# A mixture-of-experts layer on one core: expert rows written plainly to a place of their own, with an eleventh weight buffer

## What is computed

```python
x = x + concat(y_ssd, y_s5) @ w_out                  # x1 below
x = x + _hier_moe(_rmsnorm(x, norm_ffn), ...)        # then a final RMSNorm

def _hier_moe(x, ...):       # coarse top-1 of 4 groups, top-2 of the 8 experts inside it
    ...
    for e in range(32):      # w_gate, w_up: 1024 x 512, w_down: 512 x 1024, each 2 MB
        h = silu(t @ w_gate[e]) * (t @ w_up[e])
        out = out + gates[:, e:e + 1] * (h @ w_down[e])
```

## Time and profile before

| | us |
|---|---|
| runs before, three | 1048.75, 1051.2, 1053.29; median 1051.2 |
| the profiled execution, its own time | 1051.08 |
| its span, first to last instruction | 1049.2 |
| TensorE matmuls busy | 935.7 (89%) |
| VectorE, ACT, POOL busy | 434.6, 329.4, 269.8 |
| data moved by DMA | 276.98 MB, mean 264 GB/s |
| mean granted TensorE clock | 0.983 of full speed |

### The profile page before, as it was taken

One profiled execution on the slowest core, in us unless ns is written; L12 is line 12 of the kernel. 1 busy time (PEld: TensorE's weight loads), 2 busy tenths in 40 slices (PEclk: granted clock), 3 DMA queues, 4 the chain that ended last, 5 costly groups with the idle time before them and its releaser, 6 DMA issues. The chain is left out here.

```text
span 1049.2 us, 17043 instructions
## 1 busy us (share of the span) xinstructions
PE 935.7 (89%) x6336; PEld 668.2 (64%) x6337; DVE 434.6 (41%) x759; ACT 329.4 (31%) x670; POOL 269.8 (26%) x511
## 2 busy tenths in 40 slices
PE   6999999999999999999899999998778777887880
PEld 5889778877786789998765555554344343444440
DVE  6999977344557879763531111110110101110112
ACT  3025323453324785223212322222212112122125
POOL 1000788888521010000022222222112121122112
PEclk9999999999999999999999999999999999999995
DMA  7586073121099748375699999999999999999984
GB/s 271 122 141 99 24 121 89 41 63 42 31 178 221 233 141 320 90 259 201 245 354 366 376 394 392 374 402 392 385 405 408 388 406 410 412 413 415 425 346 164
DMA packets 86815, 276.98 MB, mean 264 GB/s; under 512 B 37272, under 2 KB 55576, under 8 KB 69872
## 3 DMA queue, kind: packets, MB, share of 16 engines
q1 hardware_dynamic: 75616, 250.27, 66.6%
q0 software_dynamic: 8800, 19.60, 6.8%
q10 hardware_dynamic: 2352, 6.47, 1.6%
HBM read 260.04 MB, written 25.68 MB: 272 GB/s over the span
## 5 line engine op out<-in xcount | busy, mean ns | idle before, releaser
L689 PE MATMUL ps<-sb_arena 128*128 128x260 f32 (+2 forms) x1152 | 265.6, 391 | 10.0 <-DMA sb_arena<-wi 9.1
L689 PEld LDWEIGHTS ps<-sb_arena 128*128 128x128 f32 x1152 | 219.9, 192 | 55.2 <-DMA sb_arena<-wi 9.3
L2018 DVE TENSOR_TENSOR sb_s5b<-sb_s5b,ps 128x256 f32<-128x256 f32 x34 | 21.1, 620 | 404.5 <-PE ps L1062 404.5
L1076 PE MATMUL ps<-sb_arena 128*64 128x512 f32 x544 | 127.6, 612 | 23.1 <-DVE sb_arena L2022 23.1
L1062 PE MATMUL ps<-sb_arena 128*64 128x256 f32 x1088 | 124.2, 381 | 23.5 <-DMA sb_arena<-w_up 23.5
L1055 PE MATMUL ps<-sb_arena 128*64 128x256 f32 x1088 | 124.2, 381 | 23.2 <-DMA sb_arena<-w_gate 22.5
L1055 PEld LDWEIGHTS ps<-sb_arena 128*64 128x64 f32 x1088 | 78.1, 137 | 80.3 <-DMA sb_arena<-w_gate 38.0
L1062 PEld LDWEIGHTS ps<-sb_arena 128*64 128x64 f32 x1088 | 77.4, 137 | 67.7 <-DMA sb_arena<-w_up 32.1
L1440 ACT ACTIVATE sb_kxf<-ps,sb_gate_of 64x512 f32<-64x512 f32 x36 | 24.6, 682 | 281.0 <-PE ps L1076 280.2
L1076 PEld LDWEIGHTS ps<-sb_arena 128*64 128x64 f32 x544 | 39.0, 139 | 89.8 <-issue 58.9
L654 POOL COPY sb_rwc<-sb_tok_of 64x1 int32 x36 | 6.5, 180 | 320.3 <-ACT sb_kxf L1441 320.2
(11 more groups left out here) (310 smaller groups left out, 1229.3 us busy)
## 6 DMA issues: line engine op xcount, KB each, us to landing
sb_arena<-w_up SPq DMA_DIRECT2D x32, 2048.0 KB, 40.8
sb_arena<-w_gate SPq DMA_DIRECT2D x32, 2048.0 KB, 41.0
sb_arena<-w_down SPq DMA_DIRECT2D x32, 2048.0 KB, 41.0
sb_arena<-wi SPq DMA_DIRECT2D x28, 512.0 KB, 3.9
sb_arena<-w_out SPq DMA_DIRECT2D x16, 512.0 KB, 4.1
sb_arena<-ssm_in POOLq DMA_DIRECT2D x8, 512.0 KB, 9.2
sb_arena<-wglu SPq DMA_DIRECT2D x8, 512.0 KB, 5.0
o_ssm_s<-sb_arena POOLq DMA_DIRECT2D x8, 512.0 KB, 4.5
```

What stands on the lines that cost most here:

```text
L689: last = mm(ps[:, b0 + h, 0:t1 - t0], ring[w % 3][:, k, :], src[:, k, t0:t1], start=k == 0, stop=k == KD - 1)
L1076: last = mm(ps[64 * r:64 * r + 64, 4, :], ht[:, k % 2, 64 * (k // 2):64 * (k // 2) + 64], Wd[s][:, k, 512 * r:512 * r + 512], start=k == 0 ...
```

## The change

- Each pair of a token and a choice has its own row in `out_scr` (1040 rows): 2 x token + choice. The scatter is a plain write there, nothing is added in DRAM, and `sum_scr` with its five stores goes. The destinations `dst_of` come from one more one-hot product (ten matmul records, `tab_mm` now counts four) and three small VectorE operations.
- x1 is evicted times 0.5 (`x1_rows`, and `ssum` is doubled for it), and at a tile's eviction the gathered rows of x1/2 are added to both choices' rows. ACT evicts one half of the tile; VectorE evicts the other with the add in one operation, then adds to ACT's half. `yadd` takes the place of `yev` for TensorE and POOL. VectorE's loop now also runs in rings of four.
- A gather may only overwrite `xg` when that add is done, so POOL now scatters tile q first and then gathers tile q+4. `xg` and `yo` move to `kxf`, two buffers to a column, on partitions 0 to 63 and 64 to 127. The first gathers wait for `x1t_mm` 10 and, from the third on, `tab_mm` 4.
- The space of `xg` becomes part of the up buffers: `Wu_first` serves expert 0, and with it the up weights run one expert ahead like the gate weights. The order of the loads becomes down(e), gate(e+1), up(e+1).
- At the end each block is loaded with both of its rows (4.26 MB in all), and VectorE adds the two (`both_rows`) before the square.

```diff
-        sum_scr = scratch("sum_scr", [NT, D])
+        out_scr = scratch("out_scr", [2 * NT, D])
...
-        Wg_first = part(4096, KD, FF)
-        xg = [part(18544 + 1024 * i, D, p=(0, T)) for i in range(RING)]
+        Wg_first, Wu_first = part(4096, KD, FF), part(26736, KD, FF)
...
-        yo = [kxf[0:T, D + 1024 * u:D + 1024 * u + 1024] for u in range(2)]
+        side = [slice(0, T), slice(T, 2 * T)]
+        xg = [kxf[side[u % 2], 2 * D * (u // 2):2 * D * (u // 2) + D] for u in range(RING)]
+        yo = [kxf[side[u], D:2 * D] for u in range(2)]
...
@@ SP, before the loop and in it
-            sp.dma_start(Wu[2], usrc[2]).then_inc(wu_ld[2], 16)
-            sp.wait_ge(sum_st, 80)
+            sp.dma_start(Wu[1], usrc[2]).then_inc(wu_ld[1], 16)
+            sp.wait_ge(x1t_mm, 9)
+            sp.dma_start(Wu[2], usrc[3]).then_inc(wu_ld[2], 16)
+            sp.wait_ge(xs_st, 80)
             sp.wait_ge(x1t_mm, 10)
             sp.dma_start(Wd_to[2], dsrc[2]).then_inc(wd_ld[2], 16)
...
-                    load_expert(s, of(usrc, e), of(dsrc, e), bass.ds(e - (WBUF - 1), 1))
-                    load_gate(s, of(gsrc, e + 1), bass.ds(e - (WBUF - 2), 1))
+                    load_down(s, of(dsrc, e), bass.ds(e - (WBUF - 1), 1))
+                    load_gate_up(s, of(gsrc, e + 1), of(usrc, e + 1), bass.ds(e - (WBUF - 2), 1))
...
-                sp.dma_start(G[i][0:n, 0], sum_scr[t0:t0 + n, :]).then_inc(gy[i], 16)
+                sp.dma_start(G[i][0:n], out_scr[2 * t0:2 * (t0 + n), :].rearrange("(t k) d -> t k d", k=2)).then_inc(gy[i], 16)
@@ POOL, the loop
-                    pl.wait_ge(staged, it * RING + u + 1)
+                    nc.gpsimd.tensor_copy(rwc[u % 2], dst_of[:, bass.ds(it * RING + u, 1)]).then_inc(rwc_done, 1)
+                    pl.wait_ge(rwc_done, it * RING + u + 1)
+                    pl.wait_ge(yadd, it * RING + u + 2)
                     pl.nop(nofuse=True)
+                    scatter(u % 2, yo[u % 2], rwc[u % 2])
+                    pl.wait_ge(yst[(u + 1) % 2], (it * 2 + (u + 1) // 2) * 16 + 16 * ((u + 1) % 2))
+                    pl.nop(nofuse=True)
+                    pl.sem_inc(yo_free, 1)
...
+                    gather(u, idc[u])
@@ TensorE
+            for j in range(1, 10, 2):
+                last = mm(ps[0:T, 7, 0:IDXC], oh_row[:, j, :], oh_tok[:, j, :], start=j == 1, stop=j == 9)
+            last.then_inc(tab_mm, 1)
...
-                    pe.wait_ge(yev, q + 1)
+                    pe.wait_ge(yadd, q + 1)
@@ ACT
-                    act_(yo[u % 2][:, 0:512], ps[0:64, 4, :], ACT.Copy, scale=gate_of[0:64, bass.ds(q, 1)])
-                    act_(yo[u % 2][:, 512:1024], ps[64:128, 4, :], ACT.Copy,
-                         scale=gate_of[64:128, bass.ds(q, 1)]).then_inc(yev, 1)
+                    far, cols = side[1 - u % 2], slice(512 * (1 - u % 2), 512 * (1 - u % 2) + 512)
+                    act_(yo[u % 2][:, cols], ps[far, 4, :], ACT.Copy, scale=gate_of[far, bass.ds(q, 1)]).then_inc(yev, 1)
@@ VectorE, in the loop behind the three operations of before
+                    dv.wait_ge(staged, q + 1)
+                    dv.wait_ge(gath[u], it * 16 + 16)
+                    dv.wait_ge(yo_free, q + 1)
+                    dv.wait_ge(dmm, q + 2)
+                    V.scalar_tensor_tensor(yo[u % 2][:, cols], ps[near, 4, :], gate_of[near, bass.ds(q, 1)], xg[u][:, cols],
+                                           ALU.mult, ALU.add)
+                    dv.wait_ge(yev, q + 1)
+                    V.tensor_tensor(yo[u % 2][:, others], yo[u % 2][:, others], xg[u][:, others], ALU.add).then_inc(yadd, 1)
@@ VectorE, at the end
+            def both_rows(j):
+
+                i = LAST[j]
+                n = TR[i][1]
+                dv.wait_ge(gy[i], 16)
+                V.tensor_tensor(G[i][0:n, 0], G[i][0:n, 0], G[i][0:n, 1], ALU.add).then_inc(sum_ready, 1)
```

More of the change, by code:

```diff
@@ L334, in build @@
             "idc_done", "staged", "xtr", "xev", "gmm", "umm", "silu", "hr", "htr", "hev", "dmm", "yev"))
-        rwc_done, yst, yo_free = sem("rwc_done"), sem("yst"), sem("yo_free")
-        sum_st = sem("sum_st")
+        rwc_done, yadd, yo_free = sem("rwc_done"), sem("yadd"), sem("yo_free")
+        yst = [sem(f"yst{i}") for i in range(2)]
+        dst_done, sum_ready = sem("dst_done"), sem("sum_ready")
         gy = [sem(f"gy{i}") for i in range(5)]
@@ L630, in _, with gather, scatter @@
                 pl.dma_start(hout[b], h0b[b]).then_inc(h0s_st[b % 2], 16)
+            def gather(u, index):
+                nc.gpsimd.indirect_dma_start(xg[u], None, x_scr, bass.IndirectOffsetOnAxis(ap=index, axis=0),
+                                             bounds_check=NT - 1, oob_is_err=False).then_inc(gath[u], 16)
+            def scatter(u, rows_, index):
+                nc.gpsimd.indirect_dma_start(out_scr, bass.IndirectOffsetOnAxis(ap=index, axis=0), rows_, None,
+                                             bounds_check=2 * NT - 1, oob_is_err=False).then_inc(yst[u], 16)
             pl.wait_ge(tab_ev, 1)
             pl.wait_ge(xs_st, 80)
[L634 to L637, removed]
+            pl.wait_ge(x1t_mm, 10)
+            gather(1, tok_of[:, 1:2])
+            gather(0, tok_of[:, 0:1])
+            pl.wait_ge(tab_mm, 4)
+            gather(2, tok_of[:, 2:3])
+            gather(3, tok_of[:, 3:4])
+            pl.wait_ge(dst_done, 1)
             pl.wait_ge(gath[0], 16)
-            nc.gpsimd.indirect_dma_start(sum_scr, bass.IndirectOffsetOnAxis(ap=tok_of[:, IDXC - 1:IDXC], axis=0), xg[0], None,
-                                         bounds_check=NT - 1, oob_is_err=False, compute_op=ALU.add).then_inc(yst, 16)
+            scatter(1, xg[0], dst_of[:, IDXC - 1:IDXC])
             nt = tile_bound(pl, slice(E, E + 1), E)
@@ L648, in _ @@
                     pl.nop(nofuse=True)
[L649 to L660, removed]
+                    gather(u, idc[u])
             for u in range(RING):
                 pl.wait_ge(gath[u], ((nt + RING - 1) // RING) * 16 + 16)
-            pl.wait_ge(yst, ((nt + RING - 1) // RING) * RING * 16 + 16)
+            for u in range(2):
+                pl.wait_ge(yst[u], ((nt + RING - 1) // RING) * 32 + 16 * u)
             pl.nop(nofuse=True)
@@ L1044, in x_transposes, with expert @@
                 x_turn(xst)
-            def expert(gate_w, gate_ld, gate_turn, s, turn, q0, q1):
+            def expert(gate_w, gate_ld, up_w, up_ld, gate_turn, s, turn, q0, q1):
                 with pe.Fori(q0, q1) as q:
@@ L1409, in _ @@
             act_(rdif, rdif, ACT.Exp).then_inc(r_out, 1)
-            for i, (t0, n) in enumerate(TR):
-                ac.dma_start(sum_scr[t0:t0 + n, :], x1[i][0:n]).then_inc(sum_st, 16)
             ac.wait_ge(x1t_mm, 10)
@@ L1417, in _ @@
             nt = tile_bound(ac, slice(E, E + 1), E)
-            for s_, v_ in ((silu, 1), (yev, 1), (yo_free, 1)):
+            for s_, v_ in ((silu, 1), (yo_free, 1)):
                 ac.sem_inc(s_, v_)
-            ac.wait_ge(tab_mm, 3)
+            ac.wait_ge(tab_mm, 4)
             act_(root_of, ps[0:T, 5, T:T + IDXC], ACT.Copy)
@@ L2025, in _ @@
-            dv.sem_inc(hr, RING - 1)
+            dv.sem_inc(yadd, 1)
+            with dv.Fori(0, (nt + RING - 1) // RING) as it:
+                for u in range(RING):
+                    q = it * RING + u
+                    dv.wait_ge(yadd, q + 1)
+                    dv.wait_ge(silu, q + 2)
+                    dv.wait_ge(umm, q + 1)
+                    dv.wait_ge(htr, q + 1)
+                    V.tensor_tensor(hh.rearrange("p (j c) -> p c j", j=2), sg.rearrange("p (c j) -> p c j", j=2),
+                                    ps[:, 1, 0:256].rearrange("p (c j) -> p c j", j=2), ALU.mult).then_inc(hr, 1)
+                    dv.wait_ge(htr, q + 2)
+                    dv.wait_ge(dmm, q + 1)
+                    V.tensor_copy(ht.rearrange("p a b -> p (a b)"), ps[:, 3, 0:256]).then_inc(hev, 1)
+                    dv.wait_ge(xtr, q + 3)
+                    V.tensor_tensor(xt, ps[:, 2, :].rearrange("p (k t) -> p k t", k=KD), bc(g8, 2, T), ALU.mult).then_inc(xev, 1)
+                    near, cols = side[u % 2], slice(512 * (u % 2), 512 * (u % 2) + 512)
+                    others = slice(512 * (1 - u % 2), 512 * (1 - u % 2) + 512)
+                    dv.wait_ge(staged, q + 1)
[6 more added lines that the diff above has]
+                    V.tensor_tensor(yo[u % 2][:, others], yo[u % 2][:, others], xg[u][:, others], ALU.add).then_inc(yadd, 1)
@@ L2033, in _ @@
             dv.wait_ge(moe_ld, 80)
+            both_rows(0)
             mean_square(0)
```

78 lines of the change are left out of this document (38 added, 40 removed).

## The result

| | kernel before | changed kernel |
|---|---|---|
| median of 20 runs | 1053.07 us | 1057.82 us |
| lowest, highest | 1048.75, 1059.27 | 1052.47, 1064.1 |
| ratio of the runs | | 1.0046, interval 1.003 to 1.0062 |
| profiled execution, span | 1051.08, 1049.2 | 1054.63, 1052.7 |

The changed kernel is 0.46% slower, 4.8 us, just inside the 0.5% that the prediction called no change, where 1043.1 us was forecast with 0.60 on faster; 1057.8 us also lies outside the range of 1037 to 1052. The interval leaves out 1, so the loss is real. Both profiled executions are among the faster ones of their kernels. The first half of the two programs does the same work and ends at a different time in each profile, so from here on times within a profile are counted from **t0**, SP's issue of the w_down load behind the last block of the projection (L516 before, L518 after).

A forecast was written before the change was run, and what follows sets the result against it. The experts' weights on saturated DMA were taken to set the loop's pace, so DMA work removed moves its end one for one: 1051.1 - 11.0 (plain rows) - 2.5 (start) + 5.5 (tail) = 1043.1 us, range 1037 to 1052.

The forecast's parts named there:

- Step 1: Expert loop: plain scatter rows instead of adding rows on POOL's queue q0 save 11.0 us, between 9.8 and 14.6.
- Rival B: Scatter rows cost POOL's queue the same whether they add or not; 1054.1 us, chance 0.12.
- Step 2: Start of the expert loop: stores gone and an eleventh load; -3.5 backlog, +0.7 table matmuls, +0.3 gather, in all -2.5 us.
- Rival C: Loop start: first gather takes 9 to 10 us beside w_down, TensorE waits about 4 us; 1047 us, chance 0.15.
- 4.1 us of backlog: Loop start: w_down of expert 3 could land after 7.6 us, not 11.7; at most 4.1 us gained, 3.5 taken.
- Step 3: Expert loop: the new order of loads and the waits for the add cost nothing.
- Step 4: Tail after the last matmul: extra loads and VectorE adds per block cost +5.5 us, between 3.5 and 7.
- Rival D: Expert loop: weights also run faster without adding rows, 1.4% or 6 us more; 1037 us, chance 0.18.
- three signs of being wrong: q0's share stays, DMA stops being full between 600 and 1000 us, or the tail is as short as before.
- the expected profile: New profile: q0 at 4.5 to 5%, no early TensorE gather wait over 1 us, last matmul near 1010 us, tail about 31.

The follow-up runs named there:

- b_plain: Kernel before with only the add taken from its scatters, so the sum over choices is left out; ratio 0.9897 with the kernel before.
- a_acc_root: a_both_root with scatters adding in DRAM again, on rows that two copies of the input tokens fill first; ratio 1.004 with the kernel before.
- a_both_root: Changed kernel with w_down of expert 2 and up of expert 3 held until the first gather landed, and root before square; ratio 0.9939 with the kernel before.
- a_up_late: Changed kernel with the up load of expert 3 put behind the x_scr stores and w_down of expert 2; one run, 1048.72 us.
- a_up_root: a_root_first with up of expert 3 moved behind the x_scr stores and w_down of expert 2; ratio 0.9945 with the kernel before.
- a_ten_root: a_both_root with the up weights of expert 3 issued only once expert 0's up matmuls are done; ratio 0.9938 with the kernel before.
- a_root_first: Changed kernel with ACT taking the root of block j before the square of block j+1 in the tail; ratio 0.9995 with the kernel before.
- a_best: a_both_root with up of expert 3 issued once the x_scr stores landed, before the first gather, w_down of expert 2 behind it; ratio 0.9941 with the kernel before.
- a_down_late: Changed kernel with w_down of expert 2 held until the first gather landed, the up load left in place; one run, 1049.79 us.
- a_both_late: Changed kernel with w_down of expert 2 and up of expert 3 held until the first gather landed; ratio 1.0003 with the kernel before.

## Why the prediction was wrong, point by point

**Step 1, plain rows: right.** 11.0 us were forecast out of 9.8 to 14.6. The timed pairs give 10.8 (b_plain) and 10.6 us (a_acc_root against a_both_root); q0 gave up 10.4 us of its share; the profiles show 7.6 and 8.4 us at the last matmul. Rival B, with 0.12, is refuted.

**Step 2, the start: wrong in sign, and the step that failed.** The text had "That is just in time ... I take 0.3 us". It had seen that the stores run behind four loads and put the gather near t0 + 29 (536.7); it left at t0 + 30.1. It then gave the gather 4.8 us to land, the time of a gather without a load beside it, although its own sum let w_down leave at the same moment. It took 9.5 us. Rival C had this right in kind ("it shares the engines with w_down") but was given 0.15 and 4 us. What it cost was 6.3 us of stall, 0.7 us of table matmuls and 1.5 us of the clock that fell behind the stall, which neither the forecast nor rival C had: w_down of expert 3 left 8.2 us later, and landed 4.3 us later, not 2.5 us earlier. Moving one load (a_up_late) brings the last matmul from 515.6 to 508.2.

**The 4.1 us of backlog did not show.** 3.5 of them were in the sum. The queue was empty ahead of w_down of expert 3, as step 2 said; but a_up_root, where it landed in 8.0 us at t0 + 49.7, is no faster than a_ten_root, where it landed in 12.4 at t0 + 53.8; the two intervals leave room for some 3 us at the most. What became of these 4 us in the stream was not followed further.

**Step 3, the waits in the loop: right, but for a small one.** No wait of the loop's add shows on TensorE. Its waits in the changed kernel between 850 and 950 us (in total, times, longest, us):

```profile
PE ps L1071 <- DMA sb_arena<-w_gate: 7.9, 7, 1.3
PE ps L1078 <- DMA sb_arena<-w_up: 7.4, 6, 1.2
PE ps L1092 <- DVE sb_arena L2045: 4.1, 5, 1.2
PE ps L1092 <- DMA sb_arena<-w_down: 0.9, 1, 0.9
```

The two weights that come last lead, as before; the third line is the down product waiting for its own input, not for a row that is written out, and the kernel before has it too (5.9 us in the same stretch). The fourth is new: from the first loop load to the end of the loop TensorE waits 4.1 us for w_down, in four pieces, before in none. The new order of the loads, in which w_down no longer comes behind the up weights of its expert, is the likely reason; no run takes it by itself. Yet TensorE's waits for all weights together fall from 46.0 to 42.6 us, so no loss by the order shows in the sum.

**Step 4, the tail: the size right by luck, as two errors cancel.** +5.5 forecast, +6.0 measured. The last scaling ended at 28.7 us behind the last matmul, not 24.9: the step "the last block needs the square and root between" applied that chain to the last block only, while ACT's order, square before root, makes it hold for each block but the last, whose scaling follows 1.82 us behind. Against it, the last store and the end took 3.1 us, not 6.3 (25.8 less 19.4 is 6.4 in the kernel before). They took 3.2 to 3.4 us in four profiles with scalings 2.59 apart, 4.5 and 4.6 in two others (a_acc_root, a_both_root), and 6.4 and 6.7 (b_plain) with scalings 1.45 apart. That stores close together get in each other's way fits these numbers; no run shows it by itself. That it was ACT's order is shown by a_root_first.

**The sum.** From t0 in the profiles: landing of the first loop load +4.3, the stream -4.4, the tail +6.0, together +5.9; t0 itself was 2.4 us earlier in the profile of the changed kernel, which gives the +3.5 between the spans. The stream's 4.4, against b_plain's 7.2, leaves 2.8 us, which lies within the 3 us by which this stretch scatters from profile to profile. Rival D had asked for faster weights (its 1.4% of 470 us is 6.6, not 6); they did not come: q1 took 2.46 us per MB before (94.0% of 473 us for 180.63 MB) and 2.47 after.

Against -8.0 forecast the profiles give +5.9, 13.9 us too much: 6.8 at the start (+4.3 for -2.5), 6.6 in the stream (-4.4 for -11.0) and 0.5 in the tail. In absolute time 1.9 us more come from the kernel before, 1053.07 us in twenty runs and 1051.2 in three. The start is the part that the experiments trace to a cause. Of the stream's 6.6 us, 3.8 are missing in b_plain's profile too, whose timed runs do give 10.8; this stays open. None of the three signs of being wrong came: q0's share fell, the DMA engines stayed full (1.01 from 560 to 1010 us), and the tail grew. The sign that did speak was the expected profile's "No early TensorE wait on the first gather of over 1 us".

## What to carry to other kernels

When a change takes work off a saturated DMA stretch, look at the point where the stretch begins: whatever the first dependent tile needs there (here 64 gathered rows of 4 KB) may stand behind one bulk load that is needed only later and beside another, and its landing time is to be taken from rows with the same traffic beside it. Two delays in a row may each be nearly harmless and together a stall, so price the sum of them against the cover, the work that the waiting engine has to do anyway. In a tail of short steps across two engines, write down the program order of both engines before pricing a spacing; here one swap of root and square was worth 5.4 us.

## What was not expected of the hardware

- After a stall of 6.3 us on TensorE the granted clock was 0.50, and the 16 down matmuls that followed took 5.20 us, not 3.65; after 1.5 us of waiting they took 4.85 (a_best), but after 2.0 us in two pieces 3.65 (a_down_late). The one-hot product behind 2.5 to 3.1 us without a matmul took 3.65 us in eight profiles and 5.35 in one (a_both_late). So the length of one wait doesn't tell whether the clock falls.
- A gather of 64 rows landed in 3.7 us with no load beside it (a_both_late), in 9.5 us beside one of 2 MB (the changed kernel), and in 8.4 us beside two that had left just ahead of it (a_up_late).
- The last store and the end took 3.1 us with stores 4 us apart, and 6.4 us with stores 1.4 us apart.
